# Attention over pairs of heads: score matmuls in row halves, value matmuls in column halves, the negated shift formed with the mask

## The chip, the cores and the metric

The kernel runs on one core of a Trainium2 chip. The metric is the device time of one execution in microseconds (us).

## The reference

Two layers (DEPTH = 2) over 256 tokens of width 1024, all in float32. Each layer is a gated feed-forward block, a mixer and a second feed-forward block, each with an RMS norm and a shift, scale and gate computed from a conditioning vector. The change lies in the attention inside the mixer:

```
o_a = banded_attention(qa, ka, v, A_WINDOW, a_sinks)          # 4 heads, window 128, a sink logit per head
o_b = causal_attention([q_nope, q_pe], k_b, v_b)              # 4 heads of 96 for scores, 64 for values
o_cmp, o_slc = nsa_compressed_selected(qc, qc_rot, k_cmp, v_cmp, k_slc, v_slc)   # 8 heads
o_win = banded_attention(qc_rot, k_win, v_win, C_WINDOW)      # 8 heads, window 256
o_c = g0 * o_cmp + g1 * o_slc + g2 * o_win
out = concatenate([o_a, o_b, o_c]) @ w_out
```

At 256 tokens the selection takes every block and the window of 256 covers everything, so "slc" and "win" are causal attention with different keys and values, 64 wide.

## The kernel before, in words

Feed-forward and output projections run as three float32r matmuls of split operands (high and low parts), scores, transposes and value matmuls as plain float32, which TensorE runs as two passes each (the trace shows two instructions; a transpose is one). Each engine has its own instruction list, written out by hand; counting semaphores tie the lists together.

The attention of a layer is a loop over 24 JOBS, one head each: four "a" heads, four "b" heads, then for each of eight C heads a "slc" and a "win" job. On TensorE iteration n does scores(n), turn_probs(n - 2), values(n - 3) and part of the output projection of a finished pair of heads (mix_out). Names in it:

- scores: two matmuls into bank n % 2 of PSUM (tensor ps), queries 0 to 127 against keys 0 to 127, queries 128 to 255 against all 256 keys. A head's queries and keys lie in one half of the partitions (64 of 128 rows), those of a b head in 96 rows. For 16 of the jobs (MIX_SUM) a transpose of a piece of accm rides in the same bank; its sums are the modulation of the next block.
- VectorE reduces masked scores to a maximum and writes them to E (in sq), then forms the negated scaled maximum in stat (lines 1605 to 1614). ScalarE takes the exponentials (1086, 1088); VectorE normalises (1624 to 1630).
- turn_probs: three transposes of the probabilities into bank 2; ScalarE copies them to ET (1076).
- values: the value matmuls write 64 partitions of bank 3 (one half of the columns of the array), two heads sharing the bank. A "win" job adds the compressed branch, a matmul over 32 rows (733).
- After a pair's last job VectorE splits bank 3 into uh and ol (1590, 1592); round_tall and rest_tall split the rows of w_out (957, 1345), round_wide and rest_wide those of the next feed-forward (950, 1316).
- compressed_probs: the softmax of the compressed branch for all heads, eight operations on VectorE, in iteration 1.
- link: a VectorE operation followed by a wait for its own end.

## Time and profile before

| | us |
|---|---|
| median of 3 runs | 1241.76 |
| range | 1240.63 to 1242.49 |
| the profiled execution | 1242.38 |
| its span | 1240.5 |
| TensorE matmuls busy | 1167.3 (94%) |
| VectorE busy | 863.0 (70%) |
| ScalarE busy | 463.7 (37%) |

The granted clock over the span is 0.968 of full speed. The two attention loops lie at 341.7 to 434.0 and 945.7 to 1038.0. In a row of the timeline the first number is the start, the second the length; "64*128 64x128 x2" is two instructions with a stationary operand on 64 rows by 128 columns of the array; what stands in brackets at the end is the engine's idle time before the row and what ended it. Matmuls overlap their neighbours by their latency, so their price is read from start to start.

### The profile page before, as it was taken

To read this page: it belongs to the slowest core of one execution; us is meant where nothing else is said; L and a number is where in the kernel's file an instruction comes from. 1 tells how busy PE (TensorE), PEld (TensorE's weight loads), DVE (VectorE), ACT (ScalarE), POOL (GpSimd) and SP (SyncE) were. 2 spreads that over 40 slices of the span, in tenths; PEclk is the share of its full clock that TensorE was granted. 3 is DMA by queue.
4 is the path that set the end of the run, shared out by engine and by line. 5 is a ranking of instruction groups with operands and counts; after the bars stand their busy time and mean duration, and the time that the engine had idled before them with its cause. 6 is when DMAs were issued, how large, how long until landed. Compare 5 with 4: busy or idle time off the path is not lost.

```text
span 1240.5 us, 13541 instructions
## 1 busy us (share of the span) xinstructions
PE 1167.3 (94%) x5135; PEld 874.6 (71%) x5135; DVE 863.0 (70%) x1625; ACT 463.7 (37%) x789; POOL 25.8 (2%) x30
## 2 busy tenths in 40 slices
PE   2899999999989989999989999999998998999998
PEld 1678887656556568888767888775654655888877
DVE  6887777658677678666477777858676777665544
ACT  2444333211255454434244343422114554444332
POOL 6100000000000000000000000000000000000000
PEclk9899999997989999999999999999887999999999
DMA  9899886476402029877347988874562110777641
GB/s 362 279 388 338 304 311 219 149 199 203 137 1 68 35 88 385 292 274 255 119 164 282 372 317 311 311 233 136 136 203 68 35 34 35 250 243 227 214 136 68
DMA packets 153461, 253.70 MB, mean 205 GB/s; under 512 B 9638, under 2 KB 128052, under 8 KB 145204
## 3 DMA queue, kind: packets, MB, share of 16 engines
q1 hardware_dynamic: 152692, 251.53, 59.3%
q10 hardware_dynamic: 704, 1.30, 0.3%
q8 instruction: 41, 0.67, 0.2%
q14 instruction: 24, 0.20, 0.0%
HBM read 251.76 MB, written 1.05 MB: 204 GB/s over the span
## 4 chain that ended last, share of the span: by engine, by line
PE 79%; DVE 13%; DMA 4%; ACT 2%; issue 1%; SPq 1%; DVEq 0%; ACTq 0%
PE ps L580 11%; PE ps L578 11%; PE ps L579 11%; PE ps L683 8%; PE ps L599 6%; PE ps L603 6%; PE ps L601 6%; DMA ada<-in_ada_w_dram 4%; PE ps L561 3%; PE ps L727 2%; DVE wlo L1316 2%; PE ps L793 2%; PE ps L590 2%; PE ps L692 1%; DVE acc L1289 1%; DVE h L1339 1%
## 5 line engine op out<-in xcount | busy, mean ns | idle before, releaser
L578 PE MATMUL ps<-wh,uh 128*128 128x512 f32 x640 | 252.9, 395 | 0.0
L580 PE MATMUL ps<-wlo,uh 128*128 128x512 f32 x640 | 249.8, 390 | 0.0
L579 PE MATMUL ps<-wh,ul 128*128 128x512 f32 x640 | 249.5, 390 | 0.0
L1316 DVE TENSOR_TENSOR wlo<-wide,wh 128x1024 fp32r<-128x1024 f32 x176 | 207.5, 1219 | 6.5 <-ACT wh L950 5.1
L950 ACT CAST wh<-wide 128x1024 fp32r<-128x1024 f32 x176 | 176.0, 1048 | 11.6 <-DMA wide<-in_ffn_w_in_dram 11.6
L1410 DVE TENSOR_TENSOR fa<-fs,ps 128x512 f32<-128x512 f32 x44 | 30.3, 688 | 206.0 <-ACT fs L980 205.6
L980 ACT ACTIVATE fs<-ps 128x512 f32<-128x512 f32 x44 | 26.3, 597 | 341.9 <-PE ps L580 328.2
L599 PE MATMUL ps<-th,fh 128*128 128x512 f32 x352 | 140.9, 400 | 0.0
L580 PEld LDWEIGHTS ps<-wlo,uh 128*128 128x128 f32 x640 | 120.2, 188 | 25.4
L603 PE MATMUL ps<-tlo,fh 128*128 128x512 f32 x352 | 138.0, 392 | 0.0
L601 PE MATMUL ps<-th,fl 128*128 128x512 f32 x352 | 137.6, 391 | 0.0
L579 PEld LDWEIGHTS ps<-wh,ul 128*128 128x128 f32 x640 | 120.4, 188 | 24.0
L578 PEld LDWEIGHTS ps<-wh,uh 128*128 128x128 f32 x640 | 120.3, 188 | 23.7
L1345 DVE TENSOR_TENSOR tlo<-tall,th 128x1024 fp32r<-128x1024 f32 x104 | 123.2, 1220 | 7.4 <-ACT th L957 7.3
L683 PE MATMUL ps<-wide,u 128*128 128x512 f32 (+2 forms) x320 | 126.4, 555 | 0.0
L957 ACT CAST th<-tall 128x1024 fp32r<-128x1024 f32 x104 | 104.5, 1050 | 8.4 <-DMA tall<-in_ffn_w_out_dram 8.4
L1327 DVE SCALAR_TENSOR_TENSOR acc<-ada,cond,acc 128x2048 f32<-128x2048 f32 (+1 forms) x49 | 100.1, 2042 | 7.7 <-DMA ada<-in_ada_w_dram 7.4
L683 PEld LDWEIGHTS ps<-wide,u 128*128 128x128 f32 x320 | 61.7, 195 | 59.6 <-issue 54.2
L601 PEld LDWEIGHTS ps<-th,fl 128*128 128x128 f32 x352 | 66.7, 189 | 14.3 <-issue 1.0
L599 PEld LDWEIGHTS ps<-th,fh 128*128 128x128 f32 x352 | 66.6, 189 | 14.1 <-issue 1.0
L603 PEld LDWEIGHTS ps<-tlo,fh 128*128 128x128 f32 x352 | 66.4, 189 | 14.2
L962 ACT CAST fh<-ps 128x512 fp32r<-128x512 f32 x44 | 25.8, 587 | 69.8 <-PE ps L590 69.8
(248 smaller groups left out, 1350.0 us busy)
## 6 DMA issues: line engine op xcount, KB each, us to landing
wide<-in_ffn_w_in_dram SPq DMA_DIRECT2D x176, 512.0 KB, 5.2
ada<-in_ada_w_dram SPq DMA_DIRECT2D x60, 1024.0 KB, 7.9
tall<-in_ffn_w_out_dram SPq DMA_DIRECT2D x44, 1024.0 KB, 6.8
wide<-in_w_in_dram SPq DMA_DIRECT2D x14, 1024.0 KB, 7.8
tall<-in_w_out_dram SPq DMA_DIRECT2D x8, 1024.0 KB, 7.5
ada<-in_ada_w_dram SPq DMA_DIRECT2D x16, 512.0 KB, 5.9
wide<-in_c_cmp_w_dram SPq DMA_DIRECT2D x4, 1024.0 KB, 10.3
wide<-in_w_in_dram SPq DMA_DIRECT2D x4, 832.0 KB, 8.2
```

The lines of the kernel that those rows point to most:

```text
L578: mm(o, uh[:, k, rows_], wh[:, hsl, :, k, :], start=(k == 0), stop=False, skip_group_check=True)
L579: mm(o, ul[:, k, rows_], wh[:, hsl, :, k, :], start=False, stop=False, skip_group_check=True)
L580: i = mm(o, uh[:, k, rows_], wlo[:, s, :, k, :], start=False, stop=(k == KD - 1), skip_group_check=True)
L599: mm(y[:, t, hf, :], hi[:, toks], th[:, slot, a, cols], start=(first and x == 0), stop=False, skip_group_check=True)
L601: mm(y[:, t, hf, :], lo[:, toks], th[:, slot, a, cols], start=False, stop=False, skip_group_check=True)
L603: i = mm(y[:, t, hf, :], hi[:, toks], tlo[:, slot, a, cols], start=False, stop=(last and x == len(rows) - 1), skip_group_check=True)
L683: i = mm(ps[:, banks + t, 0:width], u[:, k, t * P:(t + 1) * P], wv[:, k, :], start=(k == 0), stop=(k == KD - 1))
L950: nc.scalar.copy(wh[:, (n + 1) % 2, :, 2 * c:2 * c + 2, :], raw).then_inc(wh_ready, 1)
L957: nc.scalar.copy(th[:, n % 2, m % 2, :], tall[:, n % 2, m % 2 * DM:(m % 2 + 1) * DM]).then_inc(th_ready, 1)
L1316: tt(wlo[:, n % 2, :, ks, :], raw, wh[:, (n + 1) % 2, :, ks, :].bitcast(F32), ALU.subtract)\
L1327: stt(part, piece, cond[:, k:k + 1], part, ALU.mult, ALU.add).then_inc(ada_used, 1)
L1345: tt(tlo[:, n % 2, m % 2, :], tall[:, n % 2, m % 2 * DM:(m % 2 + 1) * DM], th[:, n % 2, m % 2, :].bitcast(F32), ALU.subtract).then_inc(tl_ ...
```

## The change

The loop goes over 12 UNITS, pairs of heads: a0, a1, b0, b1, and for each pair of C heads "slc" and "win". Both heads' scores are issued together, into banks 0 and 1, with neighbouring matmuls on different row halves (for b heads one head after the other). Both heads' values are issued together, neighbouring matmuls on different column halves. A "win" unit issues one head's compressed matmul ahead of the values and the other's behind them. TensorE's iteration n is scores(n), values(n - 2), turn_probs(n - 1, 0), mix_out, turn_probs(n - 1, 1). The reduction works with the scale -scale and a minimum, started from the negated sink for a heads, so it yields the negated shift itself. E has four slots instead of three, the second ET lies in the tensor rows. compressed_probs moves to iteration 0, ahead of the first normalisation.

```diff
-JOBS = [("a", h) for h in range(A_H)] + [("b", h) for h in range(B_H)]
-JOBS += [(br, h) for h in range(C_H) for br in ("slc", "win")]
-NJ = len(JOBS)
-LAST = [n for n in range(NJ) if JOBS[n][1] % 2 and (n + 1 == NJ or JOBS[n + 1][1] != JOBS[n][1])]
+UNITS = [("a", p) for p in range(A_H // 2)] + [("b", p) for p in range(B_H // 2)]
+UNITS += [(br, p) for p in range(C_H // 2) for br in ("slc", "win")]
+NU = len(UNITS)
+LAST = [n for n in range(NU) if UNITS[n][0] != "slc"]
...
-MIX_SUM = range(3, 19)
-PRE_HI = {12: 0, 13: 1, 16: 2, 17: 3}
-PRE_LO = {13: 0, 14: 1, 17: 2, 18: 3}
+MIX_SUM = range(2, 10)
+PRE_HI = {7: 0, 8: 1, 9: 2, 10: 3}
+PRE_LO = {8: 0, 9: 1, 10: 2, 11: 3}
...
+        nsink = sb("nsink", [P, A_H])
...
-        E = sq[:, 0:1152].rearrange("p (r n) -> p r n", r=3)
-        ET = sq[:, 1152:1920].rearrange("p (r n) -> p r n", r=2)
+        E = sq[:, 0:1536].rearrange("p (r n) -> p r n", r=4)
+        ET = (sq[:, 1536:1920], rows[:, :, :].rearrange("p r n -> p (r n)"))
...
             def scores(l, n):
-                q, k, _, _, _ = job(n)
-                bank = ps[:, n % 2, 0:3 * P]
-                if n >= 2:
-
-                    pe.wait_ge(nm_ready, l * NJ + (n - 1))
-                mm(bank[:, 0:P], q[:, 0:P], k[:, 0:P], start=True, stop=True, skip_group_check=True)
-                i = mm(bank[:, P:3 * P], q[:, P:2 * P], k[:, :], start=True, stop=True, skip_group_check=True)
+                if n >= 1:
+
+                    pe.wait_ge(nm_ready, head_at(l, n - 1, 1))
+                order = [(i, t) for i in range(2) for t in range(NT)] if UNITS[n][0] == "b" else \
+                    [(i, t) for t in range(NT) for i in range(2)]
+                for i, t in order:
+                    q, k, _, _, _ = head(n, i)
+                    lo, hi = ((0, P), (P, 3 * P))[t]
+                    x = mm(ps[:, i, lo:hi], q[:, t * P:(t + 1) * P], k[:, 0:hi - lo], start=True, stop=True,
+                           skip_group_check=True)
+                    if t == 1 and n not in MIX_SUM:
+                        x.then_inc(s_ready, 1)
                 if n in MIX_SUM:
-                    v = MIX_SUM.index(n)
                     pe.wait_ge(accm_ready, l + 1)
-                    i = tr(ps[:, n % 2, 3 * P:4 * P], accm[:, v * P:(v + 1) * P], ident)
-                i.then_inc(s_ready, 1)
-
-            def turn_probs(l, n):
-
-                pe.wait_ge(en_ready, l * NJ + (n + 1))
-                if n >= 1:
-                    pe.wait_ge(et_ready, l * NJ + n)
+                    for i in range(2):
+                        v = 2 * MIX_SUM.index(n) + i
+                        tr(ps[:, i, 3 * P:4 * P], accm[:, v * P:(v + 1) * P], ident).then_inc(s_ready, 1)
+
+            def turn_probs(l, n, i):
+
+                pe.wait_ge(en_ready, head_at(l, n, i))
+                if n or i:
+                    pe.wait_ge(et_ready, head_at(l, n, i) - 1)
                 for b in range(3):
-                    i = tr(ps[:, 2, b * P:(b + 1) * P], E[:, n % 3, b * P:(b + 1) * P], ident)
-                i.then_inc(pt_ready, 1)
+                    x = tr(ps[:, 2, b * P:(b + 1) * P], E[:, n % 2 * 2 + i, b * P:(b + 1) * P], ident)
+                x.then_inc(pt_ready, 1)
 
             def values(l, n):
-                _, _, v, _, _ = job(n)
-                br, hh = JOBS[n]
-                o = ps[64 * (hh % 2):64 * (hh % 2) + 64, 3, 0:SEQ]
-                pair = sum(m < n for m in LAST)
-                first = n == 0 or JOBS[n - 1][1] != hh
-                if first and hh % 2 == 0 and pair:
-                    pe.wait_ge(o_ready, l * 8 + pair)
-                pe.wait_ge(et_ready, l * NJ + (n + 1))
-                mm(o, v(0), ET[:, n % 2, 0:SEQ], start=first, stop=False, skip_group_check=True)
-                i = mm(o[:, P:SEQ], v(1), ET[:, n % 2, SEQ:3 * P], start=False, stop=False, skip_group_check=True)
+                br, pair = UNITS[n]
+                first, last = br != "win", br != "slc"
+                done = sum(m < n for m in LAST)
+                o = [ps[64 * i:64 * i + 64, 3, 0:SEQ] for i in range(2)]
+                v = [head(n, i)[2] for i in range(2)]
+                if first and done:
+                    pe.wait_ge(o_ready, l * 8 + done)
+
+                def compressed(i):
+                    r = slice(32 * ((2 * pair + i) % 4), 32 * ((2 * pair + i) % 4) + 32)
+                    return mm(o[i], vrep[r, pair // 2, :], cmpT[r, pair // 2, :], start=False, stop=True,
+                              skip_group_check=True)
+
+                pe.wait_ge(et_ready, head_at(l, n, 1))
                 if br == "win":
-                    r = slice(32 * (hh % 4), 32 * (hh % 4) + 32)
-                    if hh == 0:
+                    if pair == 0:
                         pe.wait_ge(*aux_done("cmpt", l))
-                    i = mm(o, vrep[r, hh // 4, :], cmpT[r, hh // 4, :], start=False, stop=True, skip_group_check=True)
-                i.then_inc(pv_ready, 1)
+                    compressed(0)
+                for i in range(2):
+                    mm(o[i], v[i](0), ET[i][:, 0:SEQ], start=first, stop=False, skip_group_check=True)
+                for i in range(2):
+                    x = mm(o[i][:, P:SEQ], v[i](1), ET[i][:, SEQ:3 * P], start=False, stop=last, skip_group_check=True)
+                if br == "win":
+                    x = compressed(1)
+                x.then_inc(pv_ready, 1)
...
-                for n in range(NJ + 3):
-                    if n < NJ:
-                        if n in (0, A_H, A_H + B_H):
-
-                            pe.wait_ge(*aux_done({0: "ka", A_H: "kb1", A_H + B_H: "kw"}[n], l))
+                for n in range(NU + 3):
+                    if n < NU:
+                        if n in (0, 2, 4):
+
+                            pe.wait_ge(*aux_done({0: "ka", 2: "kb1", 4: "kw"}[n], l))
                         scores(l, n)
-                    if 0 <= n - 2 < NJ:
-                        turn_probs(l, n - 2)
-                    if n >= 3:
-                        values(l, n - 3)
-                    if n == 4:
+                    if n == 2:
 
                         pe.wait_ge(prep, prep_at(l, "cmp"))
                         turn(l, "cmpt", [(g * SEQ + t * P, cp[:, t, 4 * g:4 * g + 4, :].rearrange("p a n -> p (a n)"))
                                          for g in range(2) for t in range(NT)])
+                    if 0 <= n - 2 < NU:
+                        values(l, n - 2)
+                    if 0 <= n - 1 < NU:
+                        turn_probs(l, n - 1, 0)
                     for k in range(KD):
 
-                        parts = 2 if JOBS[LAST[k]][0] in "ab" else 4
+                        parts = 1 if UNITS[LAST[k]][0] in "ab" else 2
                         for part in range(parts):
-                            if n == min(LAST[k] + 5 + part, NJ + 2):
+                            if n == min(LAST[k] + 3 + part, NU + 2):
                                 mix_out(l, k, part, parts)
+                    if 0 <= n - 1 < NU:
+                        turn_probs(l, n - 1, 1)
...
+                for n in range(NU + 1):
+                    for i in range(2):
+                        if n < NU:
+
+                            act.wait_ge(nm_ready, head_at(l, n, i))
+                            st = stat[:, n % 2 * 2 + i, :]
+                            e = E[:, n % 2 * 2 + i, :]
+                            if UNITS[n][0] == "a":
+                                hh = 2 * UNITS[n][1] + i
+                                A(st[:, 6:8], st[:, 2:4], ACT.Exp, bias=gn[:, G_SINK + hh:G_SINK + hh + 1])
+                            A(e[:, 0:P], e[:, 0:P], ACT.Exp, bias=st[:, 2:3], scale=-1.0, accum_out=st[:, 4:5])
+                            A(e[:, P:3 * P], e[:, P:3 * P], ACT.Exp, bias=st[:, 3:4], scale=-1.0,
+                              accum_out=st[:, 5:6]).then_inc(exp_ready, 1)
+                        if n >= 1:
+                            act.wait_ge(pt_ready, head_at(l, n - 1, i))
+                            if n >= 2:
+                                act.wait_ge(pv_ready, unit_at(l, n - 2))
+                            nc.scalar.copy(ET[i], ps[:, 2, 0:3 * P]).then_inc(et_ready, 1)
                     for k in range(KD):
-                        if n == min(LAST[k] + 3, NJ + 1):
+                        if n == min(LAST[k] + 1, NU):
...
-                        V.tensor_tensor_reduce(E[:, n % 3, 0:P], bank[:, 0:P], cst[:, C_CAUSAL:C_CAUSAL + P], 1.0, -3e38,
-                                               ALU.add, ALU.max, st[:, 0:1])
-                        link(V.tensor_tensor_reduce(E[:, n % 3, P:3 * P], bank[:, P:3 * P], job(n)[3], 1.0, -3e38,
-                                                    ALU.add, ALU.max, st[:, 1:2]))
-                        if br == "a":
-                            sink = gn[:, G_SINK + hh:G_SINK + hh + 1].broadcast_to([P, 2])
-                            link(stt(st[:, 0:2], st[:, 0:2], scale, sink, ALU.mult, ALU.max))
-                            ts(st[:, 2:4], st[:, 0:2], -1.0, None, ALU.mult).then_inc(nm_ready, 1)
-                        else:
-                            ts(st[:, 2:4], st[:, 0:2], -scale, None, ALU.mult).then_inc(nm_ready, 1)
...
+                link(ts(nsink[:, :], gn[:, G_SINK:G_SINK + A_H], -1.0, None, ALU.mult))
+                for n in range(NU + 2):
+                    if n < NU:
+                        br = UNITS[n][0]
+                        for i in range(2):
+                            scale = head(n, i)[4]
+                            st = stat[:, n % 2 * 2 + i, :]
+                            e = E[:, n % 2 * 2 + i, :]
+                            least = nsink[:, 2 * UNITS[n][1] + i:2 * UNITS[n][1] + i + 1] if br == "a" else 3e38
+                            dve.wait_ge(s_ready, head_at(l, n, i))
+                            if n in MIX_SUM:
+                                v = 2 * MIX_SUM.index(n) + i
+                                V.tensor_reduce(msum[:, v:v + 1], ps[:, i, 3 * P:4 * P], AX.X, ALU.add)
+                            if n >= 2:
+                                dve.wait_ge(pt_ready, head_at(l, n - 2, i))
+                            V.tensor_tensor_reduce(e[:, 0:P], ps[:, i, 0:P], cst[:, C_CAUSAL:C_CAUSAL + P], -scale, least,
+                                                   ALU.add, ALU.min, st[:, 2:3])
+                            V.tensor_tensor_reduce(e[:, P:3 * P], ps[:, i, P:3 * P], head(n, i)[3], -scale, least,
+                                                   ALU.add, ALU.min, st[:, 3:4]).then_inc(nm_ready, 1)
+                    if n == 0:
+                        compressed_probs()
+                    if n - 2 in LAST:
+                        pair = LAST.index(n - 2)
+                        dve.wait_ge(pv_ready, unit_at(l, n - 2))
                         V.tensor_copy(uh[:, pair, :], ps[:, 3, 0:SEQ]).then_inc(oh_s, 1)
...
+                    for k in range(KD):
+                        if n == min(LAST[k] + 2, NU):
+                            rest_tall(l, 1, k)
+                    if n == 2:
                         out_of(l, "cmpt", cmpT[:, :, :])
-                    for k in range(KD):
-                        if n == min(LAST[k] + 4, NJ + 2):
-                            rest_tall(l, 1, k)
                     if n in PRE_LO:
                         rest_wide(l, 1, 0, PRE_LO[n])
+                    if n == MIX_SUM[-1]:
+                        dve.wait_ge(chain_s, chain["n"])
+                        unit(msum[:, :], l, 2).then_inc(mod_ready, 1)
+                    if n < NU:
+                        for i in range(2):
+                            br, hh = UNITS[n][0], 2 * UNITS[n][1] + i
+                            st = stat[:, n % 2 * 2 + i, :]
+                            e = E[:, n % 2 * 2 + i, :]
+                            dve.wait_ge(exp_ready, head_at(l, n, i))
+                            if br == "a":
+                                link(tt(st[:, 4:6], st[:, 4:6], st[:, 6:8], ALU.add))
+                            link(V.reciprocal(st[:, 4:6], st[:, 4:6]))
+                            if br in ("slc", "win"):
+                                g = gates[:, :, hh, 1 if br == "slc" else 2]
+                                link(tt(st[:, 4:6], st[:, 4:6], g, ALU.mult))
+                            ts(e[:, 0:P], e[:, 0:P], st[:, 4:5], None, ALU.mult)
+                            ts(e[:, P:3 * P], e[:, P:3 * P], st[:, 5:6], None, ALU.mult).then_inc(en_ready, 1)
```

On TensorE, layer 0, the rows below are one "win" job of a C head before, in the middle of the loop: its scores (ckT, crT), a transpose of accm, the three transposes of the probabilities of the job two before it (sq), the values (acc, 64 columns), the compressed matmul (cmpT, vrep) and the output projection (th, tlo):

```order
L701 MATMUL ps<-ckT,crT 128x128 [waits nm_ready]
L702 MATMUL ps<-ckT,crT 128x256
L706 MATMUL ps<-cst,accm 128x128 [waits accm_ready]
L715 MATMUL ps<-cst,sq 128x128 [waits et_ready,en_ready]
L715 MATMUL ps<-cst,sq 128x128 x2
L727 MATMUL ps<-sq,acc 64x256 [waits et_ready]
L728 MATMUL ps<-sq,acc 64x128
L733 MATMUL ps<-cmpT,vrep 64x256 [waits aux_dve]
L599 MATMUL ps<-th,uh 128x512 [waits o_ready,tl_ready]
L601 MATMUL ps<-th,ol 128x512
L603 MATMUL ps<-tlo,uh 128x512
L599 MATMUL ps<-th,uh 128x512
```

And this is a "win" unit of two heads now, at the same stage; L713 are the scores, L721 the transposes of accm, L752 and L754 the values of both heads (sq and rows are the two ETs), L743 the compressed matmuls, L729 a transpose of probabilities:

```order
L713 MATMUL ps<-ckT,crT 128x128 [waits nm_ready]
L713 MATMUL ps<-ckT,crT 128x128
L713 MATMUL ps<-ckT,crT 128x256 x2
L721 MATMUL ps<-cst,accm 128x128 [waits accm_ready]
L721 MATMUL ps<-cst,accm 128x128
L743 MATMUL ps<-cmpT,vrep 64x256 [waits et_ready]
L752 MATMUL ps<-sq,acc 64x256
L752 MATMUL ps<-rows,acc 64x256
L754 MATMUL ps<-sq,acc 64x128
L754 MATMUL ps<-rows,acc 64x128
L743 MATMUL ps<-cmpT,vrep 64x256
L729 MATMUL ps<-cst,sq 128x128 [waits et_ready,en_ready]
```

One run of scores and one of values serves two heads; what stood between the first and the second head's (other shapes of the array) now stands behind both.

On VectorE, at the start of the loop of layer 0, before: the shift of the second a head (L1605 to L1612), the normalisation of the first (L1624 to L1630), then the start of compressed_probs (gt):

```order
L1605 ISA sq,stat<-ps,cst 128x128 [waits s_ready]
L1605 ISA stat 128x1
L1607 ISA sq,stat<-ps,cst 128x256
L1607 ISA stat 128x1
L1611 SCALAR_TENSOR_TENSOR stat<-stat,gn 128x2 [waits chain]
L1612 TENSOR_SCALAR stat<-stat 128x2 [waits chain]
L1624 TENSOR_TENSOR stat<-stat 128x2 [waits exp_ready]
L1625 RECIPROCAL stat<-stat 128x2 [waits chain]
L1629 TENSOR_SCALAR sq<-sq,stat 128x128 [waits chain]
L1630 TENSOR_SCALAR sq<-sq,stat 128x256
L1574 TENSOR_SCALAR gt<-gt 128x48 [waits gate_exp]
L1575 RECIPROCAL gt<-gt 128x48 [waits chain]
```

Now: the end of the shift of the second head, all of compressed_probs (gt, fs, fa, cst), and only then the start of the first head's normalisation (L1654, L1655):

```order
L1626 ISA sq,stat<-ps,cst,nsink 128x256
L1626 ISA stat 128x1
L1597 TENSOR_SCALAR gt<-gt 128x48 [waits gate_exp]
L1598 RECIPROCAL gt<-gt 128x48 [waits chain]
L1600 MEMSET fs 128x512 [waits cmp_exp,chain]
L1601 TENSOR_REDUCE cst<-fa 128x16 [waits chain]
L1602 RECIPROCAL cst<-cst 128x16 [waits chain]
L1603 TENSOR_TENSOR cst<-cst,gt 128x16 [waits chain]
L1604 TENSOR_TENSOR fa<-fa,cst 128x2x120 [waits chain]
L1605 TENSOR_TENSOR fs<-fa,cst 128x16x15 [waits chain]
L1654 TENSOR_TENSOR stat<-stat 128x2 [waits exp_ready]
L1655 RECIPROCAL stat<-stat 128x2 [waits chain]
```

The eight operations of compressed_probs moved ahead of the first normalisation, and the two operations behind each shift are gone.

## Rows read from the trace of the kernel before

**Rows 1.** Busy time by stretches, loops of both layers (length, busy, granted clock, DMA share).

```profile
341.70:353.10 11.40, 6.43 (x29) 3.47 (x27) 8.93 (x45) 6.20 (x24) 0.00 (x0) 0.72 0.00 0
353.10:434.00 80.90, 79.32 (x372) 49.72 (x372) 57.19 (x229) 41.80 (x117) 0.00 (x0) 0.98 0.12 40
...
957.10:1038.00 80.90, 79.32 (x371) 49.71 (x371) 57.15 (x229) 41.76 (x117) 0.00 (x0) 0.97 0.12 40
```

**Rows 2.** Timeline of TensorE, start-up of layer 0 (start, length, what; idle before).

```profile
343.80 0.49 PE L701 MATMUL ps<-kaT,qaT 64*128 64x128 f32 x2 [1.12 <-DVE stat L1612]
...
345.99 0.55 PE L715 MATMUL ps<-cst,sq 128*128 128x128 f32 x3 [1.26 <-DVE sq L1630]
...
350.85 0.90 PE L715 MATMUL ps<-cst,sq 128*128 128x128 f32 x3 [2.58 <-DVE sq L1630]
```

**Rows 3.** Timeline of TensorE, a B head and then a C head.

```profile
357.55 0.39 PE L701 MATMUL ps<-kbT,qbT 96*128 96x128 f32 x2
357.77 0.60 PE L702 MATMUL ps<-kbT,qbT 96*128 96x256 f32 x2
358.21 0.28 PE L706 MATMUL ps<-cst,accm 128*128 128x128 f32 x1
...
371.06 0.48 PE L701 MATMUL ps<-ckT,crT 64*128 64x128 f32 x2
371.38 0.59 PE L702 MATMUL ps<-ckT,crT 64*128 64x256 f32 x2
371.91 0.33 PE L706 MATMUL ps<-cst,accm 128*128 128x128 f32 x1
...
372.49 0.65 PE L727 MATMUL ps<-sq,kvb 128*64 128x256 f32 x2
372.97 0.38 PE L728 MATMUL ps<-sq,kvb 128*64 128x128 f32 x2
...
374.87 0.48 PE L701 MATMUL ps<-ckT,crT 64*128 64x128 f32 x2
```

**Rows 4.** Timeline of TensorE, the compressed matmul and a wait.

```profile
392.95 0.64 PE L733 MATMUL ps<-cmpT,vrep 32*64 32x256 f32 x2
393.52 0.49 PE L701 MATMUL ps<-ckT,crT 64*128 64x128 f32 x2
...
395.81 0.65 PE L727 MATMUL ps<-sq,acc 128*64 128x256 f32 x2 [0.78 <-DVE ol L1592]
```

**Rows 5.** Timeline of VectorE, start-up and a C head.

```profile
344.98 0.16 DVE L1624 TENSOR_TENSOR stat<-stat 128x2 f32<-128x2 f32 x1 [0.29 <-ACT sq L1088]
...
345.85 0.18 DVE L1574 TENSOR_SCALAR gt<-gt 128x48 f32<-128x48 f32 x1
...
348.91 0.28 DVE L1605 CUSTOM_DVE_ANT_0 sq<-ps,cst 128x128 f32<-128x128 f32 x1
...
374.08 1.22 DVE L1345 TENSOR_TENSOR tlo<-tall,th 128x1024 fp32r<-128x1024 f32 x1
376.08 0.29 DVE L1602 TENSOR_REDUCE msum<-ps 128x1 f32<-128x128 f32 x1 [0.78 <-PE ps L706]
...
376.96 0.17 DVE L1614 TENSOR_SCALAR stat<-stat 128x2 f32<-128x2 f32 x1
377.04 0.16 DVE L1625 RECIPROCAL stat<-stat 128x2 f32<-128x2 f32 x1
...
377.89 0.42 DVE L1590 CAST uh<-ps 128x256 fp32r<-128x256 f32 x1
378.34 0.42 DVE L1592 TENSOR_TENSOR ol<-ps,uh 128x256 fp32r<-128x256 f32 x1
```

**Rows 6.** Timeline of ScalarE, a C head.

```profile
384.04 0.48 ACT L1076 COPY sq<-ps 128x384 f32<-128x384 f32 x1 [2.07 <-PE ps L715]
384.79 0.40 ACT L1086 ACTIVATE sq<-sq,stat 128x128 f32<-128x128 f32 x1 [0.28 <-DVE stat L1614]
...
385.69 1.03 ACT L950 CAST wh<-wide 128x1024 fp32r<-128x1024 f32 x1
```

64 lines of the change are left out of this document (7 added, 57 removed).

## The prediction

> **What bounds the kernel now.** I read the busy time by stretches first, then TensorE's timeline through the attention loop, then VectorE's and ScalarE's beside it. The attention loop of layer 0 runs from 341.7 to 434.0, that of layer 1 from 945.7 to 1038.0: two equal pieces of 92.3 us. In each, the first 11.4 us are a start-up in which TensorE is busy for 6.4 us only and the granted clock is 0.72 on average, so more than half of them pass at the lower of its two levels (1.2 of 2.4 GHz). The other 80.9 us have TensorE busy for 79.3 and VectorE for 57.2 [rows 1]. So behind the start-up TensorE's own queue sets the end, and VectorE and ScalarE have a quarter to a half of their time free. The start-up is a chain: TensorE waits 1.12 us for the negated shift, then 1.26 and 2.58 us for the first two normalised heads [rows 2], 4.96 us in all.
>
> What does TensorE do in one head's 3.81 us (371.06 to 374.87)? Compare a B head, whose 96-row scores use the whole array, with a C head, whose scores use 64 of the 128 rows [rows 3]. Both run the same columns. The B head's two short score passes take 0.22 us and the two long ones 0.44 (357.55, 357.77, 358.21): 0.11 us per pass of 128 columns, 0.22 per pass of 256. The C head's take 0.32 and 0.53. The shape of the array tile changed before the first and after the last of these passes; the reader is to see that the price sits at the change, about 0.10 on its far side (the first weight load of 128 columns has nothing to hide behind) and 0.09 on its near side (the array runs empty). A change to the 64-column tile of the value matmuls costs less on the far side, since two long passes take 0.48 there instead of 0.44. So **a change of shape costs 0.19 us** ahead of a 128-column weight and **0.14 us** ahead of a 64-column one. The 32-row matmul of the compressed branch pays it again: 0.57 for two long passes (392.95 to 393.52) [rows 4].
>
> **The change, part by part.**
> *Fewer changes of shape.* Both heads of a pair are now scored together and valued together. Counted in the written order of one layer's loop, the changes of shape go from 90 to 48: those ahead of a 128-column weight from 58 to 28, those ahead of a 64-column one from 32 to 20. (Per pair of "slc" heads it is eight before and four after. A "win" pair gives two back, since one compressed matmul stands ahead of the values and one behind.) The columns streamed are the same to the last one. Gain per layer: 30 x 0.19 + 12 x 0.14 = 7.4 us.
>
> *Overlap of the two halves.* This is what the order of the new matmuls allows: neighbours use different halves of the rows (scores, ten of the twelve units, since the B heads fill 96 rows) or of the columns (values, all twelve). No two such neighbours stand side by side in the kernel before, so its trace can't say whether they run at once. Lower bound: nothing. Upper bound: each pass covers the next head's first pass. For the values of a pair (four passes of 0.22, four of 0.11: 1.32 us) a chain in which each head's two passes still follow one another takes three long passes and two short, 0.88: 0.43 saved. For the scores (also 1.32) the same chain would save up to 0.43, but each pass also needs a 128-column weight load of about 0.11, as long as the short pass itself, and if loads don't overlap only 0.2 is left; I take 0.3. That is 12 x 0.43 + 10 x 0.3 = 8.2 us per layer, against 0. I take the upper side. The row nearest to it speaks neither way, but a weight load already runs beside the matmul ahead of it where the shape stays (short passes at 0.11 a pass include the load), so the array does hold two weights.
> The Trainium skill, "TensorE: Matmul & The Clock Gate", Part 3, states that matmuls on different row or column tiles run concurrently, with 3.07x for four row tiles and 2.38x for three column tiles. No run here shows it yet. Taking 1.6x for two tiles as an estimate from that page, the overlap would be worth 10.8 us per layer instead of 8.2, and the time 1215 us.
>
> *The shift.* The new reduction forms the negated, masked and scaled score and its minimum at once, so two small operations of VectorE and one or two waits per head go. Before, a C head's shift and sum take 0.96 us (376.08 to 377.04) [rows 5], of which the last operation (376.96) and the wait ahead of it are about 0.2. 24 x 0.2 is 4.8 us of VectorE per layer, hidden under TensorE behind the start-up, worth 0.3 to 0.4 in it.
>
> *The start-up.* compressed_probs (3.06 us, 345.85 to 348.91) [rows 5] now stands ahead of the first normalisation, not behind it. TensorE has scored two units by about 345.1 and waits until VectorE has done the shifts, compressed_probs and one normalisation: the two shifts are done at about 343.9 (the first alone was at 343.80, and each gets shorter), then come 3.06, 0.87 (344.98 to 345.85) and some 0.1 until TensorE starts, so 347.9, a wait of 2.8. Its second turn waits for ScalarE's copy of the first, which is queued behind the exponentials of unit 1; those wait for VectorE's shift of unit 1, behind two normalisations: another 2.4. With the 1.1 at the shift as before that is 6.3 us against 4.96: +1.3 per layer. Since TensorE idles in the same place, I let the granted clock fall and rise as before.
>
> *New waits.* Both turns of a unit write one PSUM bank, so the second waits until ScalarE has copied the first: 0.20 until the copy starts, 0.44 for it (row 384.04: 0.48 busy) [rows 6], 0.15 back: 0.8 us. Before, a whole head's work lay between. Now a part of the output projection lies there (six or twelve matmuls at 0.23, so 1.4 or 2.7 us), except in iterations 2 and 7; in 12 and 13, which score nothing, the values wait as long. Four waits, 3.2 us. With the overlap TensorE's unit gets as short as 4.8 to 5.8 us, and VectorE's queue in iterations 9 to 11 holds per unit two shifts (0.76 each), two normalisations (0.85 each), for every second one the output split (2 x 0.42) and a rest of 1.22, and a further rest in each: up to 6.5 us [rows 5]. I allow 1.8 us of waiting. What TensorE idles there before, 80.9 - 79.3 = 1.6 us (0.78 of it at 395.81, for the output split) [rows 1, 4], goes or shrinks. Net +3.4 per layer.
>
> **The sum.** Per layer -7.4 - 8.2 + 1.3 + 3.4 = -10.9 us; twice, -21.8. The profiled execution took 1242.4 (span 1240.5 and 1.9 around it), 0.6 over the median of 1241.8. 1242.4 - 21.8 = 1220.6, or 1220 as a median.
>
> **The rivals.**
> *No overlap at all.* The halves are issued one behind the other and run so. Against it only the weight loads above. Then -7.4, +1.0 at the start-up, +2.3 of waits (four of 0.8, 0.7 of VectorE's, less 1.6): -4.1 per layer, 1233.6.
> *One kind overlaps and not the other,* or VectorE's queue eats part of it. Scores alone give about -6.8 per layer (1228), values alone -8.5 (1224.5); with both and 3 us more of waiting for VectorE -7.9 (1226). For the last speaks that VectorE's 57.2 busy us of 80.9 become some 52 of 70. Against it: its queue over iterations 4 to 11 sums to about 42 us, and TensorE's to about 44. The Trainium skill, "TensorEngine Tiling (Array Packing)", PSUM Bottleneck, warns of just this, that the copy out of PSUM binds once TensorE is faster; the mechanism is that of the VectorE row before.
> *Slower.* The pipeline is shallower: a unit is turned one iteration after it is scored, not two. If in every unit ScalarE's exponentials (0.90, 384.79 to 385.69) [rows 6] and copy (0.44) of one head come to lie on the path, that is 12 x 1.34 = 16 us per layer; with the overlap this replaces most of the 3.4 and ends near 1242 + 2 x 1.7 = 1245, without it near 1257. It decides from 0.9 us per unit on (10.9 / 12), 0.35 without overlap. Against it: between values(n-2) and the first turn of unit n TensorE has two turns, a part of the projection, the scores and values, about 5.1 us, while VectorE needs at most 0.15 + 0.9 + 1.2 + 1.2 + 0.85 = 4.3.
> *It does nothing,* were the price of a change of shape something else that stays, such as the semaphore waits at the same rows. Against it: the compressed matmul at 392.95 waits for nothing and still pays.
>
> **How the numbers follow.** Both overlaps 0.52 (1216 to 1224), one of them or VectorE in the way 0.20 (1224 to 1230), none 0.18 (1230 to 1236), a larger gain 0.02, no change 0.03, slower 0.05. The prediction is the first, 1220. The range takes in the first three, from 1215 (the clock rising earlier in the start-up, the scores saving the full 0.43) to 1235. 0.2% (2.5 us) is about what the measurement can tell from no change: faster 0.92, same 0.03, slower 0.05.
>
> **What the changed profile would show.** Each loop 81 to 82 us instead of 92.3. Score matmuls of a pair that start closer than 0.11 (short) and 0.22 (long), and value matmuls of the second head that start beside the first's second pass: if they start at full distance the overlap is not there. A first wait for the normalised head of 2.8 and one for ScalarE's copy of 2.4 in the start-up; waits of 0.8 in iterations 2, 7, 12 and 13. If iterations 4 to 11 show waits for VectorE of over 0.3 each, its queue binds. What would make the prediction wrong: no overlap, the granted clock staying at its lower level for 3 us longer behind the start-up (1.5 us per layer), or a start of the array for a half-tile that costs more than the 0.19 seen.

## The result, and the profile after

The changed kernel takes 1207.38 us (median of 4 runs, 1206.81 to 1209.92), the kernel before 1241.2: the ratio is 0.9737, with a 95% interval of 0.9717 to 0.9757. That is 12.6 us under the 1220 forecast and 7.6 under the lower end of the range. The profiled execution took 1206.92, its span is 1204.8.

Where does the gain lie? The busy times by stretches answer to [rows 1]. Each loop runs from its first score matmul to the two-column bf16 matmul of TensorE that ends it, 339.6 to 415.9 and 925.7 to 1002.5; the first 10.4 us of each are the start-up. Columns: stretch, length, then busy us and instructions of PE, PEld, DVE, ACT, POOL, the granted clock, DMA share, GB/s.

```profile
339.60:350.00 10.40, 3.48 (x24) 2.31 (x24) 7.92 (x36) 5.64 (x24) 0.00 (x0) 0.71 0.00 0
350.00:415.90 65.90, 61.01 (x376) 41.80 (x377) 53.22 (x210) 39.85 (x118) 0.00 (x0) 0.97 0.14 49
925.70:936.10 10.40, 3.49 (x24) 2.29 (x24) 7.92 (x36) 5.58 (x23) 0.00 (x0) 0.76 0.00 1
936.10:1002.50 66.40, 61.51 (x376) 42.00 (x375) 53.56 (x210) 40.23 (x118) 0.00 (x0) 0.96 0.14 48
...
339.60:415.90 76.30, 64.48 (x398) 44.11 (x399) 61.14 (x246) 45.48 (x140) 0.00 (x0) 0.93 0.12 42
```

The two loops take 76.3 and 76.8 us, where they took 92.2 each: 31.4 us of the 33.8 between the medians and of the 35.7 between the two spans. TensorE is busy for 64.5 us of the first loop instead of 85.65, with the same number of matmuls. VectorE, busy for 53.2 of the 65.9 us behind the start-up, now has a fifth of its time free and no longer more than a quarter.

TensorE's timeline shows how (start, length, what; in brackets the idle time before it and what ended it). The rows from 342.14 to 349.25 answer to [rows 2], those from 362.41 to 364.44 to the C head of [rows 3], those from 405.63 on to [rows 4].

```profile
342.14 0.93 PE L713 MATMUL ps<-kaT,qaT 64*128 64x128 f32 x8 [1.64 <-DVE stat L1626]
346.06 0.90 PE L729 MATMUL ps<-cst,sq 128*128 128x128 f32 x3 [3.00 <-DVE sq L1660]
349.25 0.87 PE L729 MATMUL ps<-cst,sq 128*128 128x128 f32 x3 [2.28 <-ACT sq L1112]
...
356.05 0.52 PE L729 MATMUL ps<-cst,sq 128*128 128x128 f32 x3 [0.66 <-ACT sq L1112]
...
362.41 0.93 PE L713 MATMUL ps<-ckT,crT 64*128 64x128 f32 x8
363.27 0.44 PE L721 MATMUL ps<-cst,accm 128*128 128x128 f32 x2
363.64 0.43 PE L752 MATMUL ps<-sq,kvb 128*64 128x256 f32 x1
363.64 0.43 PE L752 MATMUL ps<-rows,kvb 128*64 128x256 f32 x1
363.90 0.38 PE L752 MATMUL ps<-sq,kvb 128*64 128x256 f32 x1
363.91 0.38 PE L752 MATMUL ps<-rows,kvb 128*64 128x256 f32 x1
364.12 0.27 PE L754 MATMUL ps<-sq,kvb 128*64 128x128 f32 x1
...
364.44 0.55 PE L729 MATMUL ps<-cst,sq 128*128 128x128 f32 x3
...
383.61 0.52 PE L729 MATMUL ps<-cst,sq 128*128 128x128 f32 x3 [0.66 <-ACT sq L1112]
388.51 0.52 PE L729 MATMUL ps<-cst,sq 128*128 128x128 f32 x3 [0.50 <-ACT sq L1112]
396.58 0.55 PE L729 MATMUL ps<-cst,sq 128*128 128x128 f32 x3 [0.53 <-DVE sq L1660]
399.46 0.52 PE L729 MATMUL ps<-cst,sq 128*128 128x128 f32 x3 [0.94 <-ACT sq L1112]
405.63 0.40 PE L752 MATMUL ps<-sq,acc 128*64 128x256 f32 x1 [0.66 <-ACT rows L1112]
406.87 0.55 PE L729 MATMUL ps<-cst,sq 128*128 128x128 f32 x3 [0.37 <-DVE sq L1660]
409.70 0.64 PE L743 MATMUL ps<-cmpT,vrep 32*64 32x256 f32 x2 [0.57 <-ACT rows L1112]
```

The reader is to see two things. First, the value passes of the two heads (one reads `sq`, the other `rows`) start at 363.64 and 363.64, at 363.90 and 363.91: side by side, not in a staggered chain. The scores of a whole pair take 0.86 us (362.41 to 363.27) and the values of a pair 0.80 (363.64 to 364.44). That is what one head cost before (371.06 to 371.91 for the scores): two short and two long passes are 0.66, and the change of shape adds 0.19 or 0.14, as the prediction read them. Second, the three waits of the start-up, 6.92 us, and the eight short ones behind it, 4.9 us.

VectorE's timeline of the start-up answers to [rows 5]. `compressed_probs` begins at 342.00, behind both shifts, and the first normalisation at 345.07.

```profile
340.65 0.35 DVE L1624 CUSTOM_DVE_ANT_0 sq<-ps,cst,nsink 128x128 f32<-128x128 f32 x1 [1.39 <-PE ps L713]
...
340.93 0.48 DVE L1626 CUSTOM_DVE_ANT_0 sq<-ps,cst,nsink 128x256 f32<-128x256 f32 x1
...
342.00 0.18 DVE L1597 TENSOR_SCALAR gt<-gt 128x48 f32<-128x48 f32 x1
...
345.07 0.15 DVE L1654 TENSOR_TENSOR stat<-stat 128x2 f32<-128x2 f32 x1
...
397.29 0.28 DVE L1624 CUSTOM_DVE_ANT_0 sq<-ps,cst 128x128 f32<-128x128 f32 x1
```

### The profile page after: what moved, and what is told of

The parts are those of the page before. It is cut to its first block, busy times and chain, and to the rows that moved or that the text cites. A ratio compares the mean times of both kernels' runs of the same rounds, so it can differ in the third digit from the quotient of the medians.

```text
span 1204.8 us, 13482 instructions
## 1 busy us (share of the span) xinstructions
PE 1120.9 (93%) x5128; PEld 854.1 (71%) x5135; DVE 854.6 (71%) x1571; ACT 459.5 (38%) x789; POOL 25.8 (2%) x30
## 4 chain that ended last, share of the span: by engine, by line
PE 77%; DVE 14%; DMA 4%; ACT 2%; issue 1%; SPq 1%; DVEq 0%; ACTq 0%
PE ps L589 11%; PE ps L587 11%; PE ps L588 11%; PE ps L692 9%; PE ps L608 6%; PE ps L612 6%; PE ps L610 6%; PE ps L570 4%; DMA ada<-in_ada_w_dram 4%; DVE wlo L1339 2%; PE ps L816 2%; DVE tlo L1368 2%; PE ps L713 2%; PE ps L599 2%; PE ps L701 1%
## 5 line engine op out<-in xcount | busy, mean ns | idle before, releaser
L1339 DVE TENSOR_TENSOR wlo<-wide,wh 128x1024 fp32r<-128x1024 f32 x176 | 207.6, 1220 | 6.5 <-ACT wh L975 4.5
L610 PEld LDWEIGHTS ps<-th,fl 128*128 128x128 f32 x352 | 66.2, 188 | 14.2 <-issue 1.0
```

The source lines that it names most:

```text
L610: mm(y[:, t, hf, :], lo[:, toks], th[:, slot, a, cols], start=False, stop=False, skip_group_check=True)
L1339: tt(wlo[:, n % 2, :, ks, :], raw, wh[:, (n + 1) % 2, :, ks, :].bitcast(F32), ALU.subtract)\
```

## The experiments

The theory after the result: the halves overlap fully, and only that term was too small. Rivals: the gain comes from the fewer changes of shape and the shorter shift, or from something outside the loops. e1, e2 and e3 leave results of the second head out and serve as measurements of time only. In e8 and e9 TensorE's busy time includes the matmuls on zeros. The table holds each run's median, its ratio to the kernel before beside it, the lengths of its two loops, TensorE's busy time and all its waits in the loop of layer 0, and the span outside both loops.

| run | us | ratio (95%) | loops | TensorE busy | waits | outside |
|---|---|---|---|---|---|---|
| before | 1241.2 | | 92.2, 92.2 | 85.65 | 6.6 | 1056.1 |
| changed | 1207.38 | 0.9737 (0.9717 to 0.9757) | 76.3, 76.8 | 64.48 | 11.8 | 1051.7 |
| e1 | 1220.05 | 0.9838 (0.9819 to 0.9856) | 80.5, 81.1 | 70.83 | 9.7 | 1056.6 |
| e2 | 1218.32 | 0.9826 (0.9809 to 0.9842) | 83.1, 82.5 | 73.32 | 9.8 | 1049.5 |
| e3 | 1230.77 | 0.9927 (0.9906 to 0.9948) | 87.2, 87.2 | 78.64 | 8.7 | 1054.0 |
| e4 | 1210.46 | 0.9762 (0.9732 to 0.9791) | 76.8, 76.6 | 65.03 | 11.8 | 1058.8 |
| e5 | 1212.18 | 0.9755 (0.9725 to 0.9786) | 78.0, 77.8 | 64.53 | 13.5 | 1054.3 |
| e6 | 1203.98 | 0.9694 (0.9672 to 0.9716) | 74.0, 73.9 | 63.94 | 10.0 | 1051.9 |
| e7 | 1204.14 | 0.9698 (0.9675 to 0.9721) | 75.2, 75.2 | 62.87 | 12.3 | 1051.7 |
| e8 | 1207.69 | 0.9728 (0.9707 to 0.9748) | 73.9, 73.9 | 66.38 | 7.5 | 1057.6 |
| e9 | 1204.81 | 0.9709 (0.9694 to 0.9725) | 71.8, 71.8 | 64.21 | 7.4 | 1057.5 |
| e10 | 1235.2 | 0.996 (0.9945 to 0.9975) | 90.1, 91.4 | 83.94 | 6.2 | 1052.0 |
| e11 | 1199.4 | 0.9655 (0.964 to 0.967) | 72.5, 72.1 | 62.01 | 10.4 | 1056.1 |
| e12 | 1210.01 | 0.974 (0.9719 to 0.976) | 76.9, 76.3 | 65.08 | 11.8 | 1056.2 |

**e1, e2 and e3: take the overlap away.** e1 lets both heads of a pair read one half of the rows, e2 lets both write one half of the columns (the compressed matmuls keep theirs), e3 does both.

```diff
-                    q, k, _, _, _ = head(n, i)
+                    q, k, _, _, _ = head(n, i if UNITS[n][0] == "b" else 0)   # e1, e3
...
-                o = [ps[64 * i:64 * i + 64, 3, 0:SEQ] for i in range(2)]
+                o = [ps[0:64, 3, i * SEQ:(i + 1) * SEQ] for i in range(2)]    # e2, e3
```

> Changed kernel, but the scores of both heads of an a or C pair are computed from the first head's queries and keys, so both lie in the same row half and can't run side by side (the second head's result is left out: it is a copy of the first's). Theory A, the halves run wholly side by side, so a pair's scores cost what one head's do: 2 x 0.11 + 2 x 0.21 = 0.64 us more per pair, ten pairs per layer, 12.8 us in two layers, less 1 to 2 us where TensorE waits anyway: 1218 to 1219 us, and the score group 1.5 us from its start to that of the transposes behind it instead of 0.86. Theory B, the chain of the prediction (each pass covers the next head's first): 2 x 10 x 0.3 = 6 us more, 1213. Theory C, no overlap and the changes of shape are worth more than 0.14 to 0.19 each: no difference, 1207.

> Changed kernel, but the value matmuls of both heads write the same column half (second head into the free columns of the bank, so its values are missing from the output). Theory A: 0.64 us more per pair, twelve pairs per layer, 15.4 us in two layers less 1 to 2: 1221 us. Theory B, the chain: 2 x 12 x 0.43 = 10.3 us, 1217.5. Theory C: 1207.

> Both of these: scores in one row half, values in one column half; only the grouping in pairs and the shift formed with the mask are left of the change (second head's scores and values are left out). Theory A: 28 us less 3 for waits that get shorter: 1232 us, so that what is left against the kernel before is about 9 us, the prediction's case without overlap (1233.6). Theory B: 1223.5, and the changes of shape would be worth 17 us instead of 8. Theory C: 1207.

TensorE's timeline of e3, its first scores (of a0) and then the same unit as above:

```profile
340.13 1.57 PE L713 MATMUL ps<-kaT,qaT 64*128 64x128 f32 x8
...
364.74 1.57 PE L713 MATMUL ps<-ckT,crT 64*128 64x128 f32 x8
366.25 0.44 PE L721 MATMUL ps<-cst,accm 128*128 128x128 f32 x2
366.61 0.65 PE L752 MATMUL ps<-sq,kvb 128*64 128x256 f32 x2
367.10 0.59 PE L752 MATMUL ps<-rows,kvb 128*64 128x256 f32 x2
367.53 0.38 PE L754 MATMUL ps<-sq,kvb 128*64 128x128 f32 x2
367.75 0.38 PE L754 MATMUL ps<-rows,kvb 128*64 128x128 f32 x2
368.06 0.44 PE L729 MATMUL ps<-cst,sq 128*128 128x128 f32 x2
```

On one half the scores of a pair take 1.51 us (364.74 to 366.25) and the values 1.45 (366.61 to 368.06), against 0.86 and 0.80. So the overlap saves 0.65 us per pair in each: 10 x 0.65 + 12 x 0.65 = 14.3 per layer. TensorE's busy time agrees, 78.64 to 64.48. Of these 14.2 us, 3.1 come back as waits (8.7 to 11.8), and the loops get 10.9 and 10.5 shorter. By kind: values 5.7 to 6.8 per loop (e3 to e1, e2 to changed), scores 4.2 to 4.8 (e3 to e2, e1 to changed); the two loops in which the lower clock level held for 13.7 us instead of 10.2 (e2's first, e1's second) are among these. What is left without overlap, e3 against before, is 5.0 per loop. The totals came out as the first theory of each expectation had them, within 3 us.

**e4: both heads written one behind the other.** Score matmuls in the order head 0 short, head 0 long, head 1 short, head 1 long; values likewise, the L752 and L754 of one head together. (Lines stand one or two lower.)

```diff
-                order = [(i, t) for i in range(2) for t in range(NT)] if UNITS[n][0] == "b" else \
-                    [(i, t) for t in range(NT) for i in range(2)]
+                order = [(i, t) for i in range(2) for t in range(NT)]
...
                 for i in range(2):
                     mm(o[i], v[i](0), ET[i][:, 0:SEQ], start=first, stop=False, skip_group_check=True)
-                for i in range(2):
                     x = mm(o[i][:, P:SEQ], v[i](1), ET[i][:, SEQ:3 * P], start=False, stop=last, skip_group_check=True)
```

> Changed kernel with both heads' matmuls written head by head (all scores of one head, then all of the other; values likewise) and no other edit. If each half of the array takes its instructions from a short list of its own, only the neighbours at the seam overlap and most of the overlap is lost: 20 to 24 us more, 1229. If a half can run ahead of the other by four passes, nothing is lost: 1207 to 1209.

```profile
364.10 0.93 PE L712 MATMUL ps<-ckT,crT 64*128 64x128 f32 x8
364.96 0.44 PE L720 MATMUL ps<-cst,accm 128*128 128x128 f32 x2
...
365.34 0.43 PE L751 MATMUL ps<-sq,kvb 128*64 128x256 f32 x1
365.35 0.43 PE L751 MATMUL ps<-rows,kvb 128*64 128x256 f32 x1
365.60 0.38 PE L751 MATMUL ps<-sq,kvb 128*64 128x256 f32 x1
365.62 0.38 PE L751 MATMUL ps<-rows,kvb 128*64 128x256 f32 x1
365.82 0.27 PE L752 MATMUL ps<-sq,kvb 128*64 128x128 f32 x1
365.83 0.27 PE L752 MATMUL ps<-rows,kvb 128*64 128x128 f32 x1
```

In this timeline of e4 the long matmul of head 1 (`rows`, 365.35) starts 0.01 us behind that of head 0 and 0.47 ahead of head 0's short one (`sq`, 365.82), although it is written behind both. The scores take 0.86 again. So the order within a pair is worth nothing here: the loops are 76.8 and 76.6 us. What makes the gain is that the two heads stand in one group at all. The kernel before shows the same at one place, the start of its loops (see the section on the prediction).

**e5 and e10: the shift.** e5 is the changed kernel with the old maximum and its small operations, e10 the kernel before with only the new reduction.

```diff
-                            V.tensor_tensor_reduce(e[:, 0:P], ps[:, i, 0:P], ..., -scale, least, ALU.add, ALU.min, st[:, 2:3])
+                            V.tensor_tensor_reduce(e[:, 0:P], ps[:, i, 0:P], ..., 1.0, -3e38, ALU.add, ALU.max, st[:, 0:1])
...
+                                ts(st[:, 2:4], st[:, 0:2], -scale, None, ALU.mult).then_inc(nm_ready, 1)
```

> Changed kernel with the shift formed as before: maximum first, then one operation (two for a heads) that negates and scales, each behind a wait. Adds about 0.15 us of VectorE per head (0.35 for a heads). Theory A: in the start-up, where VectorE is on the path, two pairs of a heads cost up to 1 us per layer, and iterations 9 to 11, where TensorE waits for it, another 0.5: each loop 77.5 to 78 us instead of 76.5, 1210. Theory B, all hidden: loops unchanged, 1207.5.

> Kernel before with only the shift formed with the mask (negated scale, minimum, started from the negated sink), head by head as before. Theory A, in the start-up VectorE is on the path for three to four heads: 0.35 us each, loops 91 us instead of 92.2, 1239. Theory B, VectorE has room: loops within 0.3 us of 92.2, 1241.

Going back to the old form costs 1.7 and 1.0 us per loop (e5), 1.7 of waiting in layer 0 (11.8 to 13.5); the new form alone gives 2.1 and 0.8 (e10). The range of the totals of e5 overlaps that of the changed kernel, so only the loops tell. In e10's first loop the clock was at its lower level for 6.8 us instead of 10.2, so a part of its 2.1 is the clock. The shift is worth about 1.3 us per layer in the changed kernel. The total of e10, 5.7 us under the kernel before beside it, falls below both values that were expected (1239 and 1241); 2.9 of it lie in the loops, the rest outside.

**e6, e7, e8, e9 and e11: what the change left.** e6 puts `compressed_probs` behind the shifts of unit 1, e7 puts the compressed matmul of head 0 next to that of head 1. e8 fills the two long waits of the start-up with 12 and 9 matmuls on zeros. e9 has all three (its zeros are 5 ahead of the scores of unit 1, 2 ahead of the first turn and 12 ahead of the second), e11 has the edits of e6 and e7 alone.

```diff
-                    if n == 0:
+                    if n == 1:                                   # e6, e9, e11
                         compressed_probs()
...
-                    compressed(0)                                # e7, e9, e11
                 for i in range(2):
...
                 if br == "win":
+                    compressed(0)
                     x = compressed(1)
...
+                    if n == 1:                                   # e8, ahead of the first turn
+                        for _ in range(12):
+                            mm(ps[:, 3, :], zb[:, 0:P], zb[:, :], start=True, stop=True)
...
```

> Changed kernel with compressed_probs in iteration 1, behind the shifts of unit 1, instead of in iteration 0 ahead of the first normalisation. Theory A: the 3.06 us of compressed_probs leave the path: the first normalised head is awaited for about 0.5 us instead of 3.0 and the copy behind it no longer; unit 1 is normalised later but hidden by the scores of unit 2: each loop 2 to 2.5 us shorter, 1203. Theory B, the wait moves to the transposes of the compressed probabilities and to unit 1's turn: loops within 0.5 us, 1207.

> Changed kernel with both heads' compressed matmuls behind the values. They lie in different rows and columns of the array. If they run side by side, each of four units per layer saves 0.43 for the second matmul and 0.14 for a change of shape: 2.3 us per layer, less where TensorE then waits, 1203 to 1204. If they don't, only the change of shape goes: 0.6 us per layer, 1206.

> Changed kernel with 12 matmuls of zeros (bf16, 512 columns, 0.22 us each at the high clock level) ahead of the first turn and 9 ahead of the second, in the waits of 3.0 and 2.3 us; they write bank 3, which nothing uses then. If the low clock level behind the start-up (10.2 us of it in every loop) comes from TensorE's idling, it goes away: scores of unit 2 and what follows up to 354 run twice as fast, 4 us per layer less, 1199. If not, the loops keep their 76.5 us or lengthen by up to 0.5.

> Changed kernel with compressed_probs behind the shifts of unit 1, both compressed matmuls together behind the values, and matmuls of zeros in the start-up waits (5 ahead of the scores of unit 1, 2 ahead of the first turn, 12 ahead of the second). The loops of the three single edits are 2.6, 1.3 and 2.6 us shorter than 76.5. Theory A, they add up but for the low clock level, of which only 6.8 us are left in a loop with the first edit: 76.5 - 2.6 - 1.3 - 2.0 = 70.6 per loop, 1196. Theory B, one wait takes up the other's gain: 72.5 per loop, 1200.

> Changed kernel with compressed_probs behind the shifts of unit 1 and both compressed matmuls together behind the values, without the matmuls of zeros. Theory A: the loops add up, 76.5 - 2.6 - 1.3 = 72.7 us, and the stages outside of the loops, 1057.5 us with the zeros in both trials and 1049.5 to 1054.3 in most others, are back at about 1052: 1199. Theory B, the 1057.5 came by chance of when the clock falls and not with the zeros: 1199 to 1205, wherever the outside comes to lie.

TensorE's timeline of e6 has these three waits in its start-up:

```profile
341.13 0.93 PE L713 MATMUL ps<-kaT,qaT 64*128 64x128 f32 x8 [1.64 <-DVE stat L1626]
342.64 0.55 PE L729 MATMUL ps<-cst,sq 128*128 128x128 f32 x3 [0.58 <-DVE sq L1660]
346.03 0.88 PE L729 MATMUL ps<-cst,sq 128*128 128x128 f32 x3 [2.84 <-ACT sq L1112]
```

The wait of 3.00 us is down to 0.58, the next one is 0.56 longer, and each loop is 2.3 to 2.9 us shorter: the place of `compressed_probs` costs the changed kernel that much. Of this 1.8 us are waits (11.8 to 10.0). The rest goes with the clock: the lower level holds for 6.8 us of each loop here, for 10.2 in the changed kernel.

In e7 the two compressed matmuls of a pair (four passes, one row) take 0.57 us together, as long as one alone did in [rows 4]:

```profile
382.96 0.65 PE L743 MATMUL ps<-cmpT,vrep 32*64 32x256 f32 x4
383.53 0.55 PE L729 MATMUL ps<-cst,sq 128*128 128x128 f32 x3
```

TensorE is busy for 1.6 us less, of which 0.5 comes back as waiting (11.8 to 12.3); the loops get 1.1 and 1.5 shorter, where up to 2.3 were expected.

e8's busy times by stretches, about the start-up and the rest of layer 0 (its loop runs from 338.3 to 412.2):

```profile
339.00:349.40 10.40, 7.76 (x45) 4.19 (x44) 8.35 (x39) 5.59 (x24) 0.00 (x0) 1.00 0.01 2
349.40:413.00 63.60, 58.72 (x373) 39.68 (x372) 53.36 (x209) 39.73 (x116) 0.00 (x0) 1.00 0.15 51
```

The granted clock is 1.00 in both, so the lower level inside the loops did come from TensorE's waits in the start-up, and each loop is 2.4 to 2.9 us shorter, less than the 4 expected. But the median, 1207.69, is that of the changed kernel and not 1199: outside the loops its profile has 5.9 us more than that of the changed kernel, e9's 5.8. e9's loops, 71.8, lie between its two theories (70.6 and 72.5), its total, 1204.8, above both (1196 and 1200). Most of the 5.9 lies between the two loops (515.6 us instead of 509.9), where the lower level holds for 34.1 us in e8 and 23.9 in the changed kernel. e4 has 514.1 with 30.7 there without any zeros, so whether the zeros brought this or chance did stays open. e11 has no zeros and is the best version: 1199.4 us, beside e12's 1210.01 on the same chip.

**e12: the changed kernel once more,** beside e11.

> The changed kernel itself once more, for a second profile: the loops should repeat at 76.3 to 76.8 us. If the stages outside of them, 1051.7 us with 50.8 us at the low clock level in the first profile, repeat within 0.5 us, the 4.4 us that they are shorter than before (1056.1 with 59.6) belong to the change; if they move by 2 us or more with the time at the low level, they are chance.

The loops repeat (76.9 and 76.3), the rest does not: 1056.2 us outside them instead of 1051.7. The same stretch between the loops has the granted clock at 0.97 in e12 and at 0.98 in the first profile; outside the loops, within the span, the lower level holds for 61.4 us there and for 48.4 here (the 50.8 and 59.6 of the expectation also count a piece of the clock's record behind the last instruction; within the span they are 48.4 and 58.0). So 4.5 us more at the same code goes with 13.0 us more at the lower level. Over all fourteen profiles the two mostly rise together: outside the loops they take from 1049.5 us (e2, 41.1 us at the lower level) to 1058.8 (e4, 58.0).

## Why the prediction was off, step by step

- **Fewer changes of shape:** right. e3 keeps all of it and none of the overlap, and TensorE is busy for 85.65 - 78.64 = 7.0 us less. e3 also takes away the one overlap that the kernel before has, worth 0.6 us (the third point), so this term measures 7.6, where the step has 7.4.
- **Overlap of the two halves:** this step failed, in its size. That the halves overlap was right, and the side taken too; the term was 8.2 us per layer and measured 13.6 (14.2 from e3 to changed, less the 0.6 that the kernel before had). The step let "a chain in which each head's two passes still follow one another" run staggered, so that a long pass covers the other head's short one: 0.43 per pair saved for the values. But the two heads run in step, each pass beside the other head's same pass, so that a pair costs what one head costs: 0.65 saved. For the scores it took 0.3, since it doubted that the 128-column loads overlap. They do: the time in which weights are loaded in the loop goes from 55.77 (e3) to 44.11 us. Twice 5.4 us too little is 10.8 us, of a miss of 12.6.
- **The answer stood in the trace of the kernel before.** The step says that no two such neighbours stand side by side there, that its trace can't say whether they run at once and that no run shows it yet. That is wrong. At the start of each loop nothing stands between the scores of the first two a heads, which lie on different row halves; TensorE's timeline of the kernel before has them ahead of those of the third head alone:

```profile
341.75 0.50 PE L701 MATMUL ps<-kaT,qaT 64*128 64x128 f32 x4
342.07 0.61 PE L702 MATMUL ps<-kaT,qaT 64*128 64x256 f32 x4
343.80 0.49 PE L701 MATMUL ps<-kaT,qaT 64*128 64x128 f32 x2 [1.12 <-DVE stat L1612]
344.13 0.59 PE L702 MATMUL ps<-kaT,qaT 64*128 64x256 f32 x2
```

The eight passes of two heads take 0.93 us (341.75 to 342.68), the four of one head 0.92 (343.80 to 344.72), the four weight loads of the short passes 0.31 us and the two of one head 0.29, and e3 needs 1.57 for the same eight (340.13). Both heads' short passes come ahead of both heads' long ones, although they are written head by head, as in e4. So full overlap of row halves, overlapping weight loads and the freedom of the written order could all be read before the change; layer 1 shows the same (945.74, 946.06). For column halves the kernel before has no such place, and e2 was needed.
- **The bound above it:** the prediction called 0.43 an upper bound and derived it from the assumed chain. It was no bound: two halves that run fully side by side save 0.66. The Trainium skill, "TensorE: Matmul & The Clock Gate", Part 3, describes matmuls on different tiles running concurrently, and the traces agree. Its measured speedups lie below the number of tiles (3.07 for four, 2.38 for three), and so did the estimate taken from it, 1.6 for two, 10.8 us per layer; here the passes of a pair shrink from 1.32 to 0.66 us, a factor of 2.0.
- **The start-up:** +1.3 forecast, 6.92 - 4.96 = +2.0 measured. The waits of 2.8 and 2.4 were 3.00 and 2.28. The first one, taken as 1.1, is 1.64, because TensorE now waits for the shifts of two heads, and because a reduction that starts from the sink takes 0.35 and 0.48 us where 0.28 and 0.42 are the times of one that starts from a constant. The granted clock is 0.71 there, before 0.72, as assumed.
- **New waits:** the four for ScalarE's copy are there with 0.57 to 0.66 us instead of 0.8 (356.05, 383.61, 405.63, 409.70). The other four (388.51, 396.58, 399.46, 406.87) sum to 2.34, forecast 1.8. Together 4.9 of the 5.0; less the 1.6 of before, +3.3 against +3.4.
- **VectorE in the way:** in part. Two waits for it behind the start-up exceed the 0.3 that was named as the sign (0.53 and 0.37), and of the 14.2 us of overlap 3.1 go to waits of all kinds; but the 3 us beyond the forecast waits, which this rival needed, are not there: all waits are 11.8 us where 6.3 + 5.0 were forecast. Of the 4.9 us behind the start-up 4.0 end with ScalarE's copy out of PSUM (L1112) and only 0.9 with VectorE.
- **The shift:** counted as 0.3 to 0.4 per layer, worth about 1.3: in e5 the first wait alone is 2.07 instead of 1.64.
- **The sum again,** with measured terms: -7.6 - 13.6 + 2.0 + 3.3 = -15.9 per layer, and the loops show -15.7. Twice 15.9 from 1242.4 gives 1210.6; e12's median is 1210.01. The first profiled execution took 3.7 less, 1206.92, and that lies outside the loops, in code that the change does not touch: 1056.1 us before and 1051.7 after, with the lower clock level for 58.0 and 48.4 us. e12 has 1056.2 with the same kernel, so this share is no part of the change. Of the miss of 12.6, 9.6 thus lies in the loops (31.4 us gained, 21.8 forecast): 10.8 of overlap, less about 1 that the other terms gave back. The other 3 lie outside them, where e12, the same kernel, does not have them.

**The rivals.** No overlap came out as e3: 5.0 us per loop against the 4.1 worked out, 1230.8 us against 1233.6. One kind alone was given 1228 (scores) and 1224.5 (values); e2 and e1 took 1218.3 and 1220.1. The slower one did not happen: the longest wait behind the start-up is 0.94 us, once. (Its figure without overlap does not follow from its own terms: -7.4 + 1.0 + 16 is +9.6 per layer, about 1261 and not 1257.) That the change does nothing is refuted by e3, which has no overlap and still keeps TensorE busy for 7.0 us less per layer. A gain larger than the range had been given a chance of 0.02, and none of the signs of being wrong that the prediction names points that way.

## What to carry to other kernels

Two matmuls of the same length that fill half the array each, on different row halves or different column halves, are to be counted as one if they stand in one group with no wait between them; their order within it made no difference here, in groups of eight passes. (Halves of unequal length and longer groups were not measured.) Before a trace is said to be silent, look for the situation at the edges of a loop too: here its first two heads showed it. An upper bound must come from what the resource could do at best, and not from the schedule one imagines on it. When the engine that binds gets faster, count how much of the gain the next wait takes: here 3.1 of 14.2 us.

## What the runs showed of the hardware

- Two halves run in step: starts 0.00 to 0.01 us apart (363.64 to 363.91), in both directions of the split, and in fp32, where each matmul is two passes with a weight load each. A pair's scores go from 1.51 to 0.86 us, its values from 1.45 to 0.80 (e3 against changed).
- Matmuls of different halves start out of written order: in e4 head 1's long one starts 0.47 us ahead of head 0's short one, which is written before it, and the kernel before does the same at 341.75. The Trainium skill, "TensorE: Matmul & The Clock Gate", Part 3, states that matmuls start and end in program order and are never reordered. These rows differ from that, and the measurement decides.
- The compressed matmuls (32 rows, 64 columns) of two heads also run side by side: 0.57 us for both (e7, 382.96 to 383.53).
- The reduction with a start value per partition takes 0.35 and 0.48 us (340.65, 340.93), with a constant 0.28 and 0.42 (397.29, 397.50).
- With matmuls on zeros in the two long waits of the start-up the granted clock stays at 1.00 through the whole loop (e8), where the changed kernel has 10.2 us at the lower level; with the first wait cut from 3.00 to 0.58 us (e6) it is 6.8 us.
- The same kernel differs by 4.5 us between two profiles, outside the loops, along with 13.0 us more at the lower clock level. That sets how small a gain the total can show, while the loops repeat within 0.6 us.
